# Norm of the output rows moved from a closing stage into the expert blocks

## The chip, the cores and the metric

The kernel runs on one core of one Trainium2 chip. The metric is the device time of one execution in microseconds (us). Three runs of the kernel before gave 2715.66, 2713.44 and 2708.99; the median is 2713.44.

Five engines work beside each other, each through its own instruction queue in order, and wait for each other on semaphores: TensorE (PE in the profile), VectorE (DVE), ScalarE (ACT), GpSimd (POOL) and SyncE (SP).

## The reference, cut to what matters

A decoder layer over 2048 tokens of width 1024. The change touches only what follows the router: a mixture of 16 experts, two per token, then the second LayerNorm.

```
dest = pad_start[s_e] + (arange(A) - start[s_e])        # rows sorted by expert, padded to blocks of 128
def expert_block(args):
    xb, e = args
    h = jax.nn.silu(xb @ w_gate[e]) * (xb @ w_up[e])    # 128x1024 @ 1024x512, twice
    return h @ w_down[e]                                # 128x512 @ 512x1024
out = segment_sum(y_sorted * s_w[:, None], s_tok)       # each token: two rows summed
x = layer_norm(DN_ALPHA * x + g2 * ffn, ln2_g, ln2_b)   # mean, variance, scale, bias per row
```

Each token has rows in exactly two expert blocks. Its sum is complete when the later of them has been added.

## The kernel before, in words

Everything up to the router is unchanged and is left out here. The last stage is `experts_and_norm` (L1711). Its input is `u2_rows` (the rows for the experts), `acc` in HBM (already holding x, and 128 spare rows behind the 2048) and `records`: for each place of a block the token number and its gate weight.

The blocks: 128 rows each, numbered 0 to total-1 over all experts; with these inputs there are 41 blocks and none of the 16 experts is empty. Each product is made in three matmuls (high by high, high by low, low by high parts of the float32 operands), so weights and rows are split in a high part by ScalarE (a copy to fp32r) and a low part by VectorE (a subtraction).

PE, per block b: wait for `x_lo_done`, gate and up product (48 matmuls, `p_gu`), `turn_x(b+1)` (8 transposes of the next block's rows, L1873), `down` (24 matmuls for block b-1, `p_y`), then 4 transposes of h (L1915). The down product of a block is thus made one block later (`down(b)` works on the h of block b-1), and DVE evicts its result in `evict` (L2072) at the start of the block after that, scaled by the gate weight in the record.

ACT, per block (`body`): `high_h` (L1966), wait for the gate product, two Silu (L1979), `high_x(b+1)` (L1972), and in the first block of an expert `split_dn` (L1955, 4 chunks, each waiting for `down`'s chunk). After the last block of an expert `split_gu` of the next expert follows (L1946, 8 chunks).

DVE, per block: `low_h` (L2062), `evict`, two products of h (L2089), `low_x(b+1)` (L2079, which posts `x_lo_done`), in the first block `split_dn` (L2050); `split_gu` (L2043) after the last block of an expert.

POOL, per loop turn b: wait for the evicted rows `y_out`, scatter-add them into `acc` (L1823, an indirect DMA), wait for `x_turned` and gather the next rows `x_raw` (L1800, an indirect DMA), wait for both transfers, shift the `record` slots (four small copies, L1796), load the next record (L1790).

SP loads expert weights in pieces as soon as the splits have freed the raw buffer `stay`.

The closing stage: when the last scatter-adds have landed, SP loads all 16 tiles of 128 rows back from `acc` into `stay` (L1784). DVE takes the moments (L2131, L2133), subtracts the mean and multiplies by the gain (L2118); POOL makes the reciprocal deviation (L1856, L1858) and adds the bias (L1849); ACT scales (L2023), takes the moments of four tiles, and stores (L2001).

## Time and profile before

| what | us |
|---|---|
| median of three runs | 2713.44 |
| profiled execution, its own time | 2713.14 |
| its span, first to last instruction | 2711.5 |
| PE busy in the span | 2491.6 (92%) |
| DVE busy | 1443.4 (53%) |
| ACT busy | 1123.4 (41%) |
| POOL busy | 842.7 (31%) |
| mean granted TensorE clock | 0.965 of full speed |

The span is what the trace covers; the execution's own time is 1.6 us longer. The page divides the span in 40 slices of 68 us; PE reads 9 tenths in nearly all of them, and 0 in the last, which is the closing stage. In the timelines the first number is the start in us from the span's start, the second the duration; "x8" is eight instructions merged in one row, and what stands in brackets is the idle time of that engine before the row and who ended it.

### The profile page before, as it was taken

What the parts mean: (1) busy time and instruction counts of PE and PEld (TensorE: products, weight loads), DVE (VectorE), ACT (ScalarE), POOL (GpSimd) and SP (SyncE); (2) the same over time, 40 slices, a digit from 0 to 9 for tenths busy, and PEclk for the clock granted to TensorE, in tenths of its full rate; (3) what the DMA queues carried; (4) which work ended last, traced back from release to release, by engine and by line L of the source; (5) the groups of instructions that cost most, each with busy time, mean ns of one, the idle gap of its engine ahead of it and who ended that gap; (6) DMA issues with size and microseconds to landing.
All of it is one profiled execution on the core that took longest, in us unless ns stands there. A gap on an engine that the chain in (4) does not pass through costs nothing. (4 is left out here: it accounts for less than half of the span.)

```text
span 2711.5 us, 35984 instructions
## 1 busy us (share of the span) xinstructions
PE 2491.6 (92%) x12505; PEld 2081.0 (77%) x12506; DVE 1443.4 (53%) x1871; ACT 1123.4 (41%) x1846; POOL 842.7 (31%) x692
## 2 busy tenths in 40 slices
PE   5999899999999999999989989994998999999990
PEld 4788678778888888888878877884787888888780
DVE  6122156665656566665654335775446545534755
ACT  3122144554544444454542012212556545534754
POOL 2111023452222222222221345665322222322326
PEclk9999999999999999999999999996999999999995
DMA  7699676767575666585537666532567646555847
GB/s 265 232 312 314 250 231 189 250 199 233 184 224 165 227 186 218 173 270 183 171 122 239 213 182 210 187 117 108 164 180 228 207 135 204 169 145 146 266 122 263
DMA packets 258254, 548.04 MB, mean 202 GB/s; under 512 B 23716, under 2 KB 93464, under 8 KB 257496
## 3 DMA queue, kind: packets, MB, share of 16 engines
q1 hardware_dynamic: 236072, 483.07, 53.7%
q0 software_dynamic: 14720, 45.04, 7.6%
q10 hardware_dynamic: 7344, 18.35, 1.7%
q8 instruction: 73, 1.20, 0.2%
q14 instruction: 45, 0.37, 0.0%
HBM read 393.37 MB, written 153.02 MB: 202 GB/s over the span
## 5 line engine op out<-in xcount | busy, mean ns | idle before, releaser
L93 PE MATMUL mx_acc<-u_u,mx_w_hi 128*128 128x512 f32 x1792 | 571.4, 400 | 1.5 <-DMA mx_w_lo<-halves 1.5
L722 POOL TENSOR_TENSOR mx_wt<-mx_wt,mx_rest 128x127 f32<-128x127 f32 (+15 forms) x128 | 271.5, 2121 | 741.5 <-DVE mx_rest L924 741.5
L93 PEld LDWEIGHTS mx_acc<-u_u,mx_w_hi 128*128 128x128 f32 x1792 | 326.1, 190 | 65.9 <-DMA mx_w_lo<-halves 1.9
L932 DVE TENSOR_TENSOR mx_wt_lo<-mx_p_t,mx_wt_hi 128x512 fp32r<-128x512 f32 (+2 forms) x320 | 192.1, 604 | 326.4 <-ACT mx_wt_hi L887 324.5
L93 PE MATMUL mx_acc<-u_u,mx_w_lo 128*128 128x512 f32 x896 | 352.8, 394 | 0.0
L887 ACT ACTIVATE mx_wt_hi<-mx_p_t 128x512 fp32r<-128x512 f32 (+2 forms) x320 | 170.8, 534 | 405.4 <-PE mx_p_t L774 359.3
L924 DVE TENSOR_TENSOR_SCAN mx_rest<-mx_rest,mx_zero 128x128 f32<-128x128 f32 (+15 forms) x128 | 315.8, 2467 | 8.6 <-ACT mx_wt L869 8.6
L93 PE MATMUL moe_p_gu<-keep_wide_hi,moe_x_hi 128*128 128x512 f32 x656 | 262.6, 400 | 14.1 <-DVE keep_wide_lo L2043 13.0
L93 PE MATMUL moe_p_gu<-keep_wide_hi,moe_x_lo 128*128 128x512 f32 x656 | 258.1, 393 | 0.0
L93 PE MATMUL moe_p_gu<-keep_wide_lo,moe_x_hi 128*128 128x512 f32 x656 | 257.9, 393 | 0.0
L868 ACT ACTIVATE mx_rest<-mx_p_z 128x512 f32<-128x512 f32 (+2 forms) x320 | 171.0, 534 | 100.0 <-PE mx_p_z L761 58.9
L93 PEld LDWEIGHTS mx_acc<-u_u,mx_w_lo 128*128 128x128 f32 x896 | 169.8, 189 | 38.8
L774 PE MATMUL mx_p_t<-keep_ident,mx_wt 128*128 128x128 f32 x1088 | 174.5, 275 | 22.3 <-POOL mx_wt L722 15.7
L774 PEld LDWEIGHTS mx_p_t<-keep_ident,mx_wt 128*128 128x128 f32 x1088 | 134.2, 141 | 77.8 <-POOL mx_wt L722 32.7
L869 ACT ACTIVATE mx_wt<-mx_p_z 128x512 f32<-128x512 f32 (+2 forms) x320 | 171.9, 537 | 0.0
L93 PE MATMUL fr_acc<-u_u,fr_w_hi 128*128 128x512 f32 x512 | 162.0, 398 | 6.5 <-DVE fr_stage L424 6.3
L2043 DVE TENSOR_TENSOR keep_wide_lo<-keep_stay,keep_wide_hi 128x1024 fp32r<-128x1024 f32 x124 | 142.3, 1218 | 36.5 <-ACT keep_wide_hi L1946 22.3
L2089 DVE TENSOR_TENSOR moe_h<-moe_p_gu,moe_act_g 128x256 f32<-128x256 f32 x82 | 30.9, 419 | 235.8 <-ACT moe_act_g L1979 235.8
L93 PEld LDWEIGHTS moe_p_gu<-keep_wide_hi,moe_x_hi 128*128 128x128 f32 x656 | 124.8, 190 | 40.0 <-DVE keep_wide_lo L2043 13.7
L760 PE MATMUL mx_p_z<-mx_k_hi,mx_q 128*128 128x512 f32 (+2 forms) x320 | 131.2, 410 | 16.6 <-DMA mx_q<-qk_lo 11.9
L93 PEld LDWEIGHTS moe_p_gu<-keep_wide_hi,moe_x_lo 128*128 128x128 f32 x656 | 124.7, 190 | 27.1
L93 PEld LDWEIGHTS moe_p_gu<-keep_wide_lo,moe_x_hi 128*128 128x128 f32 x656 | 125.0, 191 | 25.1
(257 smaller groups left out, 5130.2 us busy)
## 6 DMA issues: line engine op xcount, KB each, us to landing
mx_w_hi<-halves SPq DMA_DIRECT2D x98, 512.0 KB, 3.8
mx_w_lo<-halves SPq DMA_DIRECT2D x98, 512.0 KB, 5.2
keep_stay<-in_w_gate SPq DMA_DIRECT2D x64, 512.0 KB, 5.3
keep_stay<-in_w_up SPq DMA_DIRECT2D x64, 512.0 KB, 6.4
keep_stay<-in_w_down SPq DMA_DIRECT2D x32, 1024.0 KB, 6.7
u_saved<-u_u SPq DMA_DIRECT2D x4, 4096.0 KB, 19.5
mx_w_mod<-in_w_ada SPq DMA_DIRECT2D x64, 256.0 KB, 5.2
gate_t<-mx_g_out SPq DMA_DIRECT2D x64, 256.0 KB, 5.1
```

Source lines behind the costliest of these rows:

```text
L93: mm = pe.matmul(out, a, b, start=first and n == 0, stop=last and n == len(pairs) - 1, skip_group_check=True)
L722: pool.tensor_tensor(wt[:, t % 2, 0:w - 1], wt[:, t % 2, 0:w - 1], rest[:, t % 2, 1:w], ALU.mult).then_inc(m["weights_done"], 1)
L760: pe.matmul(out, q, hi, start=True, stop=False, skip_group_check=True)
L774: mm = pe.transpose(p_t[:, n % TR, (j - 4 * r) * P:(j - 4 * r + 1) * P], wt[:, t % 2, j * P:(j + 1) * P], ident[:])
L868: act.activation(rest[:, t % 2, a:b], p_z[:, n % ZB, 0:b - a], ACT.Sigmoid, scale=-SCALE)
L869: act.activation(wt[:, t % 2, a:b], p_z[:, n % ZB, 0:b - a], ACT.Sigmoid, scale=SCALE).then_inc(m["z_used"], 1)
L887: act.activation(to, p_t[:, n % TR, 0:(k - j) * P].rearrange("p (j t) -> p j t", t=P), ACT.Copy).then_inc(m["hi_done"], 1)
L924: dve.tensor_tensor_scan(x[:, ::-1], x[:, ::-1], zero[:].to_broadcast([P, w]), 1.0, ALU.mult, ALU.max).then_inc(m["scan_done"], 1)
L932: dve.tensor_tensor(wt_lo[:, first:first + k - j], p_t[:, n % TR, 0:(k - j) * P].rearrange("p (j t) -> p j t", t=P), f32(wt_hi[:, first:fi ...
L2043: dve.tensor_tensor(lo, raw, f32(hi), ALU.subtract).then_inc(m["gu_lo_done"], 1)
L2089: dve.tensor_tensor(h[:, w], p_gu[:, 1, w], act_g[:, w], ALU.mult).then_inc(m["h_done"], 1)
```

## The change

POOL's loop now does more. In turn b it scatters a finished tile of rows into `out` (`store_rows`), scatter-adds the evicted rows as before, gathers the next x rows as before, makes the reciprocal deviation of the row tile that DVE has just measured (`deviation`), shifts seven record slots (two copies with a second buffer `shifted`), loads the next record, and gathers the rows that the block's scatter-add has just completed in `acc` back into SBUF (`gather_rows`). ACT scales that tile inside `body`, between the two Silu and `high_x`. DVE takes its moments and centres it between `evict` and the products of h, and adds the bias between `low_x` and `split_dn`. A token's row is thus normed and stored after each of its two blocks; the second store overwrites the first. The closing stage of 16 tiles is gone; three tiles of rows are still finished after the last block. The stage's buffers (`rows`, 16 semaphores `rows_in`, the tile moments) go, `row_in`, `row_out`, `last_in`, `last_out` take four strips of 1024 columns of `stay` that the weights leave free.

```diff
+            def add_rows(slot, done):
+                pool.indirect_dma_start(out=acc, out_offset=at(slot), in_=y[:], in_offset=None, compute_op=ALU.add).then_inc(done, 16)
+            def gather_rows(slot, to, done):
+                pool.indirect_dma_start(out=to, out_offset=None, in_=acc, in_offset=at(slot)).then_inc(done, 16)
+            def store_rows(slot, rows, done):
+                pool.indirect_dma_start(out=out_rows, out_offset=at(slot), in_=rows, in_offset=None, bounds_check=S - 1,
+                                        oob_is_err=False).then_inc(done, 16)
+            def load_clear(n):
+                past(pool, m["scaled"], n)
+                pool.dma_start(row_in, acc[S:S + P, :]).then_inc(m["row_in"], 16)
+            def deviation(n):
+                wait_apart(pool, marks["pool"], m["row_mv"], n)
+                pool.tensor_scalar(var[:, 0:1], mv[:, 0, 1:2], EPS / ALPHA ** 2, None, ALU.add).then_inc(m["row_var"], 1)
+                wait_apart(pool, marks["pool"], m["row_var"], n)
+                pool.tensor_tensor(rstd[:, 0:1], var[:, 0:1], minus_half[:], ALU.pow).then_inc(m["row_rstd"], 1)
...
             for n in (1, 2, 3):
                 load_record(n)
+                record_known(n)
                 wait_apart(pool, marks["pool"], m["x_turned"], n)
                 gather_x(n)
...
                 shift_records(n)
+                if n > 1:
+                    deviation(n - 1)
+                    load_clear(n - 1)
...
-            with pool.Fori(0, total - 3) as b:
+            def block_rows(b, c=None):
+                if c is not None:
+                    wait_apart(pool, marks["pool"], m["normed"], b + 2)
+                    store_rows(0, row_out, m["out_stored"])
                 wait_apart(pool, marks["pool"], m["y_out"], b * 2 + 6)
-                add_rows(0, y, m["y_added"])
+                wait_apart(pool, marks["pool"], m["row_in"], b * 16 + 48)
+                add_rows(2, m["y_added"])
                 wait_apart(pool, marks["pool"], m["x_turned"], b + 4)
                 gather_x(b + 4)
+                if c is not None:
+                    wait_apart(pool, marks["pool"], m["out_stored"], c * 16 + 16)
+                pool.sem_inc(m["out_free"], 1)
+                deviation(b + 3)
                 wait_apart(pool, marks["pool"], m["y_added"], b * 16 + 16)
                 pool.sem_inc(m["y_free"], 1)
                 wait_apart(pool, marks["pool"], m["x_in"], b * 16 + 80)
                 shift_records(b + 4)
                 load_record(b + 5)
+                wait_apart(pool, marks["pool"], m["scaled"], b + 3)
+                gather_rows(1, row_in, m["row_in"])
+                record_known(b + 5)
+
+            block_rows(0)
+            block_rows(1)
+            with pool.Fori(0, total - 4) as c:
+                block_rows(c + 2, c)
...                                                     # POOL after the loop
+            store_rows(0, row_out, m["last_stored"])
+            add_rows(2, m["last_added"])
+            deviation(total + 1)
+            pool.wait_ge(m["last_added"], 16)
+            gather_rows(2, row_in, m["row_in"])
+            gather_rows(3, last_in, m["last_row_in"])
+            store_rows(1, row_out, m["last_stored"])
+            deviation(total + 2)
...
+            store_rows(2, row_out, m["last_stored"])
+            pool.wait_ge(m["last_stored"], 48)
+            store_rows(3, last_out, m["last_stored"])
...                                                     # ACT
+            def scale_rows(n):
+                act.wait_ge(m["row_rstd"], n + 1)
+                act.wait_ge(m["centered"], n + 1)
+                act.wait_ge(m["out_free"], n + 1)
+                act.activation(row_out, row_in, ACT.Copy, scale=rstd[:, 0:1]).then_inc(m["scaled"], 1)
             def body(b, e, first):
                 high_h(b)
...
                     act.activation(act_g[...], p_gu[...], ACT.Silu).then_inc(m["silu_done"], 1)
+                scale_rows(b)
                 high_x(b + 1)
                 if first:
                     split_dn(e, b)
...                                                     # DVE
+            def center_rows(n):
+                dve.wait_ge(m["row_in"], n * 16 + 16)
+                for i in range(2):
+                    dve.bn_stats(stats[:, 0, i], row_in[:, i * NB:(i + 1) * NB]).then_inc(m["row_stats"], 1)
+                wait_apart(dve, marks["dve"], m["row_stats"], 2 * n + 2)
+                dve.bn_aggr(mv[:, 0], stats[:, 0].rearrange("p a b -> p (a b)")).then_inc(m["row_mv"], 1)
+                dve.wait_ge(m["row_mv"], n + 1)
+                dve.scalar_tensor_tensor(out=row_in, in0=row_in, scalar=mv[:, 0, 0:1], in1=ln_g[:], op0=ALU.subtract,
+                                         op1=ALU.mult).then_inc(m["centered"], 1)
+            def add_bias(n):
+                dve.wait_ge(m["scaled"], n + 1)
+                dve.tensor_tensor(row_out, row_out, ln_b[:], ALU.add).then_inc(m["normed"], 1)
             def body(b, e, first):
                 low_h(b)
                 evict(b)
+                center_rows(b)
...
                 low_x(b + 1)
+                add_bias(b)
                 if first:
                     split_dn(e)
```

## Rows read from the trace of the kernel before

**Rows 1.** Busy time in one stretch of expert blocks: length, engines, clock, DMA share, GB/s.
```profile
2120.00:2400.00 280.00, 280.00 (x1331) 233.09 (x1330) 138.28 (x191) 147.50 (x196) 80.30 (x112) 1.00 0.60 177
```
**Rows 2.** Chain that ended last, one block and the start of the next.
```profile
2404.59 10.94 PE moe_p_gu L93 x48
2415.53 0.87 PE moe_p_x L1873 x8
...
2422.30 10.94 PE moe_p_gu L93 x48
```
**Rows 3.** Timeline of POOL in the same block.
```profile
2417.20 0.98 POOL L1800 DMA_INDIRECT keep_x_raw<-u_rows,keep_record  x1 [4.67 <-PE moe_p_x L1873]
2421.34 0.18 POOL L1796 COPY keep_record<-keep_record 128x2 uint32<-128x2 uint32 x1 [3.16 <-DMA keep_x_raw<-u_rows,keep_record]
...
2423.96 0.58 POOL L1790 DMA_DIRECT2D keep_record<-records  x1 [1.39 <-issue]
```
**Rows 4.** Timelines of ACT and DVE in the same block.
```profile
2416.44 1.09 ACT L1972 ACTIVATE moe_x_hi<-moe_p_x 128x512 fp32r<-128x512 f32 x2 [0.22 <-PE moe_p_x L1873]
...
2417.07 1.29 DVE L2079 TENSOR_TENSOR moe_x_lo<-moe_p_x,moe_x_hi 128x512 fp32r<-128x512 f32 x2 [0.33 <-ACT moe_x_hi L1972]
```
**Rows 5.** Closing stage: timeline of POOL, then groups by line (busy us, mean ns).
```profile
2673.60 0.21 POOL L1856 TENSOR_SCALAR moe_var<-moe_mv 128x2 f32<-128x2 f32 x1
2673.90 0.71 POOL L1858 TENSOR_TENSOR moe_rstd<-moe_var,moe_minus_half 128x2 f32<-128x2 f32 x1
...
L2118 DVE SCALAR_TENSOR_TENSOR keep_stay<-keep_stay,moe_mv,moe_p_gu 128x1024 f32<-128x1024 f32 x16 | 19.5, 1242 | 0.0
L2023 ACT ACTIVATE keep_stay<-keep_stay,moe_rstd 128x1024 f32<-128x1024 f32 x16 | 17.5, 1138 | 9.2 <-POOL moe_rstd L1858 8.6 <-DVE keep_stay L2118 0.6
L2131 DVE BATCH_NORM_STATS2 moe_stats<-keep_stay 128x6 f32<-128x512 f32 x24 | 15.3, 679 | 10.4 <-DMA keep_stay<-acc 10.4
```
**Rows 6.** Change of expert after a block that began at 2587.68: ACT, DVE.
```profile
2601.92 7.70 ACT L1946 ACTIVATE keep_wide_hi<-keep_stay 128x1024 fp32r<-128x1024 f32 x8
...
2603.01 9.17 DVE L2043 TENSOR_TENSOR keep_wide_lo<-keep_stay,keep_wide_hi 128x1024 fp32r<-128x1024 f32 x8 [1.57 <-ACT keep_wide_hi L1946]
```
**Rows 7.** An expert with one block, begun at 2053.93: ACT, then the chain.
```profile
2071.24 1.06 ACT L1955 ACTIVATE moe_dn_hi<-keep_stay 128x1024 fp32r<-128x1024 f32 x1 [0.30 <-PE moe_p_y L93]
...
2075.98 13.97 PE moe_p_gu L93 x48
```
**Rows 8.** TensorE clock behind three gaps: timeline of PE, then stretches (columns of Rows 1).
```profile
507.38 0.66 PE L774 MATMUL mx_p_t<-keep_ident,mx_wt 128*128 128x128 f32 x4 [2.23 <-POOL mx_wt L722]
580.53 0.33 PE L774 MATMUL mx_p_t<-keep_ident,mx_wt 128*128 128x128 f32 x1 [2.13 <-DVE mx_wt_lo L932]
...
507.40:510.40 3.00, 3.00 (x12) 2.43 (x13) 2.17 (x3) 1.57 (x3) 0.00 (x0) 0.68 0.43 129
580.50:583.50 3.00, 2.96 (x17) 2.52 (x18) 2.33 (x3) 2.46 (x5) 1.91 (x1) 1.00 0.00 0
2076.00:2082.00 6.00, 6.00 (x14) 4.74 (x15) 6.00 (x6) 5.98 (x7) 0.58 (x1) 0.50 0.96 350
```
**Rows 9.** DMA issues after 1900 (median us to landing), and the longest wait for x.
```profile
keep_x_raw<-u_rows,keep_record POOLq DMA_INDIRECT x40, 5.1
...
POOL keep_record L1796 <- DMA keep_x_raw<-u_rows,keep_record: 170.9, 41, 6.9
```
**Rows 10.** First block of the stage: POOL's gather for block 2, then the chain.
```profile
1908.48 1.00 POOL L1800 DMA_INDIRECT keep_x_raw<-u_rows,keep_record  x1 [2.33 <-DMA keep_record<-records]
...
1912.32 10.89 PE moe_p_gu L93 x48
```
**Rows 11.** The chain at the end of the last block, and the first scatter-add behind it.
```profile
2634.90 5.46 PE moe_p_y L93 x24
...
2643.92 6.02 DMA acc<-keep_early,keep_record
```
**Rows 12.** Timeline of POOL during VectorE's split of a new expert's weights.
```profile
2606.72 0.97 POOL L1796 COPY keep_record<-keep_record 128x2 uint32<-128x2 uint32 x1 [0.17 <-POOL keep_record L1796]
```

More of the change, by code:

```diff
@@ L1520, in _ @@
             pool.wait_ge(m["scattered"], 32 * NT)
[L1521 removed]
+            pool.dma_start(record[:, SLOTS - 1], records[bass.ds(start, P), :]).then_inc(ahead["record_in"], 16)
             gain(LAST)
@@ L1836, in _ @@
                 load_record(b + 5)
-            for i in range(2):
-                wait_apart(pool, marks["pool"], m["y_out"], total * 2 + 2 * i)
-                add_rows(0, y, m["last_added"])
-                wait_apart(pool, marks["pool"], m["last_added"], 16 * i + 16)
-                pool.sem_inc(m["y_free"], 1)
-                if i == 0:
-                    shift_records(total + 1)
-            pool.wait_ge(m["last_out"], 2)
-            add_rows(1, y_last, m["last_added"])
-            def add_bias(t):
-                pool.wait_ge(m["normed"], t + 1)
-                pool.tensor_tensor(rows[:, t], rows[:, t], ln_b[:], ALU.add).then_inc(m["res_done"], 1)
@@ L1851, in _ @@
-            pool.wait_ge(m["half_set"], 1)
-            for q in range(NT // 2):
-                a, b = 2 * q, 2 * q + 2
-                pool.wait_ge(m["mv_done"], b - upto(ACT_STATS, b - 1))
-                past(pool, m["act_mv"], 2 * upto(ACT_STATS, b - 1))
-                pool.tensor_scalar(var[:, a:b], mv[:, a:b, 1], EPS / ALPHA ** 2, None, ALU.add).then_inc(m["var_done"], 1)
-                pool.wait_ge(m["var_done"], q + 1)
-                pool.tensor_tensor(rstd[:, a:b], var[:, a:b], minus_half[:], ALU.pow).then_inc(m["rstd_done"], 1)
-                for t in range(max(0, a - 2), a):
-                    if t not in DVE_BIAS:
-                        add_bias(t)
@@ L1862, in _ @@
-            for t in (NT - 2, NT - 1):
-                if t not in DVE_BIAS:
-                    add_bias(t)
+                wait_apart(pool, marks["pool"], m["scaled"], b + 3)
[5 more added lines that the diff above has]
+                block_rows(c + 2, c)
+            wait_apart(pool, marks["pool"], m["normed"], total)
+            store_rows(0, row_out, m["last_stored"])
@@ L1990, in _ @@
             high_h(total)
-            act.wait_ge(m["h_done"], 2 * total)
-            act.wait_ge(m["x_lo_done"], total + 1)
-            for row, ps in ((ln_g, p_g), (ln_b, p_b)):
-                act.activation(ps, row[:], ACT.Copy).then_inc(m["rows_copied"], 1)
-            def store(t):
-                if t in DVE_BIAS:
-                    act.wait_ge(m["res_dve"], upto(DVE_BIAS, t))
-                else:
-                    act.wait_ge(m["res_done"], t + 1 - upto(DVE_BIAS, t))
-                act.dma_start(out_rows[t * P:(t + 1) * P, :], rows[:, t]).then_inc(m["stored"], 16)
@@ L2019, in _ @@
-            moments(ACT_STATS[0])
-            for t in range(NT):
-                act.wait_ge(m["rstd_done"], t // 2 + 1)
-                act.wait_ge(m["scaled"], t + 1)
-                act.activation(rows[:, t], rows[:, t], ACT.Copy, scale=rstd[:, t:t + 1]).then_inc(m["normed"], 1)
-                if t % 3 == 1 and t // 3 + 1 < len(ACT_STATS):
-                    moments(ACT_STATS[t // 3 + 1])
-                if t >= 5:
-                    store(t - 5)
-            for t in range(NT - 5, NT):
-                store(t)
@@ L2030, in _ @@
-            act.wait_ge(m["stored"], 16 * NT)
+            scale_rows(total)
+            scale_rows(total + 1)
+            act.wait_ge(m["last_rstd"], 1)
+            act.wait_ge(m["last_centered"], 1)
+            act.activation(last_out, last_in, ACT.Copy, scale=rstd[:, 1:2]).then_inc(m["last_scaled"], 1)
         @block.vector
@@ L2138, in _ @@
-            center(NT - 1)
-            add_bias(NT - 1)
+                dve.scalar_tensor_tensor(out=y_last[:, w], in0=p_y[:, n], scalar=record[:, 3, 1:2].bitcast(F32), in1=g2r[:, w],
+                                         op0=ALU.mult, op1=ALU.mult).then_inc(m["last_done"], 1)
+                if n == 0:
+                    add_bias(total)
+            center_rows(total + 1)
+            dve.wait_ge(m["last_row_in"], 16)
+            for n in range(2):
+                w = slice(n * NB, (n + 1) * NB)
+                dve.wait_ge(m["last_done"], n + 1)
+                dve.tensor_tensor(last_in[:, w], last_in[:, w], y_last[:, w], ALU.add).then_inc(m["last_summed"], 1)
+                dve.wait_ge(m["last_summed"], n + 1)
+                dve.bn_stats(stats[:, 1, n], last_in[:, w]).then_inc(m["last_stats"], 1)
@@ new lines, in _ @@
+            dve.wait_ge(m["last_stats"], 2)
+            dve.bn_aggr(mv[:, 1], stats[:, 1].rearrange("p a b -> p (a b)")).then_inc(m["last_mv"], 1)
+            add_bias(total + 1)
+            dve.wait_ge(m["last_mv"], 1)
+            dve.scalar_tensor_tensor(out=last_in, in0=last_in, scalar=mv[:, 1, 0:1], in1=ln_g[:], op0=ALU.subtract,
+                                     op1=ALU.mult).then_inc(m["last_centered"], 1)
+            dve.wait_ge(m["last_scaled"], 1)
+            dve.tensor_tensor(last_out, last_out, ln_b[:], ALU.add).then_inc(m["last_normed"], 1)
```

114 lines of the change are left out of this document (43 added, 71 removed).

## The prediction

> **What bounds the kernel now.** I read the engines' busy time in one stretch of the expert blocks first, then the chain that ended last, then the timelines of the three engines that feed PE. In 280 us of expert blocks PE is busy 280.00 us at the full clock, while DVE is busy 138.28, ACT 147.50 and POOL 80.30 us, and the DMA engines are busy 0.60 of the time [rows 1]. So there is room beside PE on each engine by sum. The chain shows the order: a block takes 17.71 us from one gate product to the next (2404.59 to 2422.30), all of it PE, and PE finishes the transposes of the next x at 2416.40, 11.81 us into the block [rows 2]. I write S for the start of a block's gate product and S+11.8 for this point. What has to be ready at S+17.71 is `x_lo`: ACT takes 1.09 us for `x_hi` (at S+11.85) and DVE ends `x_lo` at 2418.36, S+13.8 [rows 4]. So this hand-over has 3.9 us of slack, and only that. Behind the last block the closing stage stands alone: the last PE row of the last block's down product ends at 2640.36 [rows 11], the four transposes of h behind it take 0.44 (17.71 less the 17.27 that the gate product, the transposes and the down product take [rows 2, 11]), so the last block ends at E = 2640.80, and the span at 2711.5: 70.7 us.
>
> **Removed: the closing stage.** Of these 70.7 us a part comes back, since three tiles must still be finished. Counted from E, with the same durations: the loop's last turn gathers a row tile that lands at about E+8.3 (x gather at S+12.6, landing after 5.1 [rows 9]; shift and record 3.2, from 2421.34 to 2424.54 [rows 3], less 0.3 for two copies fewer; 0.3 to the next issue, another 5.1; 17.7 of it is the block's own). The scatter-add follows 0.8 later and takes 6.0 [rows 11]: E+15.1. Two gathers, 0.8 to start, 1.3 between them and 5.1 to land: the last sum is in at E+22.3, and the other tile, 1.3 us earlier, is centred meanwhile. DVE adds the last half rows and takes their moments, four steps of 0.65 and the aggregation with its waits, about 4.5 with the centring that is still running: E+26.8. Reciprocal deviation 1.1: E+27.9. ACT scales (1.14) and DVE adds the bias (1.25) [rows 5]: E+30.4 for the first of the two tiles, the second 2.5 later and under the first one's store. Then two stores follow one after the other, since the last waits for the one before: 2 x (0.8 + 6.0), at the scatter-add's price: E+44.1. The stage shrinks by 70.7 - 44.1 = 26.6 us. A plain scatter is not in the trace; with the gather's 5.1 for it the gain is 28.4, with the longest wait of 6.9 [rows 9] for each of the five transfers in the chain about 20. I take 26.6.
>
> **Added to each block: a longer way to x_hi.** ACT works in order, and `scale_rows(b)` stands between Silu and `high_x(b+1)`. It waits for `row_rstd`, which POOL posts in `deviation`, and POOL reaches `deviation` only behind `gather_x`, which waits for PE's transposes at S+11.81. From the rows: gather starts 0.80 behind the transposes (2417.20) and ends at S+13.59 [rows 3]; 0.17 for the waits between, the two small operations end 1.01 after they begin [rows 5], S+14.77; the scaling takes 1.14, S+15.93; x_hi and x_lo end 1.92 behind the start of x_hi [rows 4], S+17.87. That is 0.18 us later than PE wants it. In a plain block PE stalls 0.2 us; there are 23 such boundaries (40 boundaries in all, less 15 changes of expert and the first two): 4.6 us. Bounds for one: 0 when the deviation takes 0.2 less, 1.0 when POOL runs beside DVE and a step takes 0.97 where 0.18 is usual [rows 12].
>
> Behind `scale_rows` and `high_x` on ACT are `split_dn`, `split_gu` and the next block's `high_h`. On DVE `center_rows` (2 x 0.68, 0.2, 1.24 [rows 5]) stands before the products of h and `add_bias` (1.25) before the splits; DVE is idle there, and the products are due only at S+17.3, so I cost both at nothing. If the rows come later than S+14 that cover is gone.
>
> **Changes of expert.** Here the 3.9 us of slack were used. Before, x_hi was done at S+12.94 [rows 4], ACT's first new chunk began at S+14.24, 1.3 later, DVE's low part 1.09 behind it, and was ready about S+16.6 (2603.01 + 1.25) [rows 6], 1.1 us before PE came. Now x_hi is done at S+17.02 (S+15.93 + 1.09), and the same 1.3, 1.09 and 1.25 follow: S+20.7. PE stalls 20.7 - 17.7 = 3.0 us. The later chunks come every 1.15 us (9.17/8), faster than PE's 1.37 (10.94/8), so the stall is paid once. 12 of the 15 changes are of this kind: 36 us. Bounds 2.5 to 4.
>
> In the other three the expert has one block only, so `split_dn` stands between. Its fourth chunk ends at S+18.37 and PE waits until S+22.05 already now [rows 7], one of three such waits in the chain. With x_hi done only at S+17.02 the four chunks of 1.06 run end to end until S+21.3: 2.9 more, 8.7 us for three.
>
> **The clock behind the stalls.** After a stall of 4.3 us the next 6 us run at a granted clock of 0.50, which is 1.2 in place of 2.4 GHz [rows 8], and the 48 matmuls take 13.97 in place of 10.94 us [rows 7, 2], 3.0 more. After 2.23 us of idling the clock fell too (0.68 over 3 us), after 2.13 us it stayed at 1.00 [rows 8]. A stall of 3.0 us lies between: bounds 0 and 3.0, I take 1.4 for each of the twelve (one short fall more often than none) and 0.5 more for the three: 18.3 us.
>
> **Start of the stage.** In the first two blocks `deviation` is not behind `gather_x` alone but behind its landing and the shift. First boundary: gather at 1908.5 [rows 10], landing 4.4 later (4.1 in rows 3), 0.7 shift, 1.1 deviation, 1.14 scaling, 1.92 x_hi and x_lo: 1917.8 against 1912.3 [rows 10]: 5.5. Second: S+11.8, 0.8, 4.4, 0.7, 1.1, 1.14, 1.92, or S+21.9 against 17.7: 4.2. Clock behind both, 1.7 each: 3.4. Together 13.1 us.
>
> **POOL's loop.** It gets a gather of rows and a store. By the working above rows land at S+26.0, which is 8.1 into the next block. The scatter-add waits for them, then 0.8 and about 1.7 of issue (less than the 2 x 1.0 of two gathers [rows 3]), and is through at 10.6, 1.2 before x's transposes. With landings of 6.9 [rows 9] this is missed. I add 0.15 us for each of 38 blocks: 5.7. The DMA load rises from 0.60 by about a quarter; no term for it.
>
> **The sum.** 13.1 + 4.6 + 36 + 8.7 + 18.3 + 5.7 = 86.4 added, 26.6 saved: +59.8. On the profiled execution's own 2713.14 (0.3 below the median) that is 2773 us, 2.2% slower.
>
> **A price from the Trainium skill.** The x gather lands 5.1 us and the scatter-add 6.0 us after its issue [rows 9, 11]. By the Trainium skill, "DMA: Bandwidth & Descriptors", section "Anatomy of one DMA - SWDGE (gpsimd) path", a transfer from the GpSimd queue takes about 2.0 us plus its bytes over 436 GB/s; for 512 KB an estimate of 3.2 us. By it the five transfers of the last chain would take some 12 us less and the two gathers of the first blocks 3 less, and the time would be about 2758; the row has a duration and stands.
>
> **Rivals.** *The rows stay hidden.* If the deviation of a tile is ready before Silu ends (S+11.6), ACT never holds x_hi and only the closing stage counts: 2713.1 - 26.6 = 2686.5, faster. It speaks for it that each engine has idle time [rows 1], against it that POOL's order places `deviation` behind a semaphore of the same block. It decides from 3.9 us: the detour adds 4.1. Chance 0.06. *Some of the stall is hidden,* so that costs and the 26.6 cancel within 8 us: 0.03. *The clock holds.* PE stalls but the clock stays at 1.00, as after 2.13 us [rows 8]: 2773 - 21.5 = 2751. Chance 0.22. *The rows set the period.* If both gathers need 6.9 us, rows land 3.6 later, 11.7 into the block, and with 2.5 of scatter-add and 0.3 behind them POOL issues the gather of x at S+14.5, not 12.6: 1.9 more on each of 38 blocks, 72 us, 2845. For it speaks that the DMA share rises, against it the median of 5.1. Chance 0.12. *DVE holds POOL.* While DVE splits a new expert's weights a POOL copy took 0.97 in place of 0.18 [rows 12, 3], one DVE operation's length and no more. If the row gather at S+21 had to wait for the whole split (9.2 from S+19.4), rows would land some 13 us into the next block and x's gather slip by 3.2 us, 15 times: 48 us, 2821. Chance 0.07.
>
> The last is a rule of the Trainium skill: "SBUF - State Buffer", section "Who interferes with whom", says that a DVE instruction with two SBUF inputs and a GpSimd instruction that reads SBUF exclude each other for the whole instruction. By that rule one instruction is waited for, as the copy shows, and nothing is added; whether an indirect DMA's index reads wait behind a row of such instructions, no trace of before shows.
>
> **Numbers.** Forecast 0.50, 2773, its own range 2755 to 2800. The range of 8 in 10 takes in the forecast and the rivals at 2751 and 2821, leaves out the two below and most of the 2845: 2735 to 2830. About 0.3% (8 us) is what a measurement of this kernel tells from no change: faster 0.06, within it 0.03, slower 0.91.
>
> **What would show it.** Right: in ACT's timeline `x_hi` starts 4 us later in each block, behind a scaling that waited for POOL's pow; PE idles about 3 us, waiting for `keep_wide_lo`, at each change of expert, with the clock at 0.50 behind most; from the last block's end 44 us remain. Wrong: ACT's scaling starts right behind Silu, blocks still 17.71 us and changes of expert without a gap; or plain blocks near 20 us, with POOL's gather of x late behind the scatter-add.

## The result and the profile after

| | before | after |
|---|---|---|
| median (four runs each) | 2713.78 | 2804.61 |
| lowest to highest | 2708.99 to 2715.66 | 2802.99 to 2807.98 |
| profiled execution, its span | 2711.5 | 2801.5 |
| mean granted TensorE clock | 0.965 | 0.959 |
| PE's first transposes of the stage (1884.3 and 1885.8 in the span) to the end E of the last block | 756.5 | 875.4 |
| of it PE idle | 17.1 | 101.3 |
| of it PE busy | 739.4 | 774.2 |
| from E to the end | 70.7 | 40.3 |

The change is slower: ratio 1.0338, 95% interval 1.0325 to 1.035. The forecast was 2773, +60; measured are +91. The last three lines say where: 84.2 us more of idle PE, 34.8 us more of PE's busy time for the same products, 30.4 us less behind the last block.

The 34.8 us are in the main two things. The 41 gate products last 25.1 us longer in sum, since 17 of them take 12.5 to 14.1 us at a lower clock (3 before). The other 9.0 us are an overlap that is gone, which the next view shows.

First the page's busy times. PE shows 33 us more than before for the same products; DVE and POOL show what was added.

```profile
PE 2524.7 (90%) x12505; PEld 2099.5 (75%) x12506; DVE 1569.6 (56%) x2039; ACT 1131.8 (40%) x1844; POOL 906.5 (32%) x750
```

The chain over one plain block and the start of the next answers to [rows 2]. The block takes 18.05 us (2066.70 less 2048.65) and not 17.71, 0.34 more. Of that 0.11 is idle time ahead of the next gate product. The rest looks like a longer gate product (11.17 in place of 10.94), but is not one.

```profile
2048.65 11.17 PE moe_p_gu L94 x48
2059.83 0.87 PE moe_p_x L1911 x8
2060.70 5.46 PE moe_p_y L94 x24
2066.16 0.44 PE moe_p_h L1953 x4
2066.60 0.11 issue
2066.70 11.17 PE moe_p_gu L94 x48
```

In the timeline of PE before, the first matmul of the gate product starts at 2404.35, 0.24 us ahead of the end of the transposes of h (2404.59). The chain books these 0.24 us with the transposes, so [rows 2] has 10.94 for a product that lasts 11.18 from its first matmul's start. That overlap is there in 37 of before's blocks and in none of after's.

```profile
2403.99 0.60 PE L1915 MATMUL moe_p_h<-keep_ident,moe_h 128*128 128x128 f32 x4
2404.35 0.48 PE L93 MATMUL moe_p_gu<-keep_wide_hi,moe_x_hi 128*128 128x512 f32 x1
```

A change of expert, as in [rows 4, 6], in the timelines of POOL, ACT, DVE and PE. The block began at 2427.36, so S+11.8 is 2439.2. Read it from the top: the gather of x, the two small operations, the scaling that waited for `rstd`, only then `x_hi`, a table load of ScalarE, the first new chunk, its low part, and PE's first matmul, 2.83 us late.

```profile
2440.25 0.99 POOL L1800 DMA_INDIRECT keep_x_raw<-u_rows,keep_record  x1 [2.16 <-PE moe_p_x L1911]
2441.26 0.28 POOL L1819 TENSOR_SCALAR moe_var<-moe_mv 128x1 f32<-128x1 f32 x1
2441.73 0.58 POOL L1821 TENSOR_TENSOR moe_rstd<-moe_var,moe_minus_half 128x1 f32<-128x1 f32 x1 [0.18 <-POOL moe_var L1819]
...
2442.34 1.15 ACT L2017 ACTIVATE keep_stay<-keep_stay,moe_rstd 128x1024 f32<-128x1024 f32 x1 [3.10 <-POOL moe_rstd L1821]
2443.40 1.06 ACT L2010 ACTIVATE moe_x_hi<-moe_p_x 128x512 fp32r<-128x512 f32 x2
2444.48 1.28 ACT L1984 ACT_TABLE_LOAD   x1
2445.78 7.69 ACT L1984 ACTIVATE keep_wide_hi<-keep_stay 128x1024 fp32r<-128x1024 f32 x8
...
2446.87 9.17 DVE L2053 TENSOR_TENSOR keep_wide_lo<-keep_stay,keep_wide_hi 128x1024 fp32r<-128x1024 f32 x8 [0.44 <-ACT keep_wide_hi L1984]
...
2448.15 0.79 PE L94 MATMUL moe_p_gu<-keep_wide_hi,moe_x_hi 128*128 128x512 f32 x1 [2.83 <-DVE keep_wide_lo L2053]
```

The table load is most of the 1.3 us that the forecast counted between `x_hi` and the first chunk. It stands there in the kernel before as well (1.28 us at 2600.63), ahead of the split. In after it lies inside the delayed chain at each change of expert; no run here moves it.

The waits of the whole stage (total us, times, longest us) hold a second story. The first two rows are the predicted one. In the third, PE waits for `x_lo`: two of the nine are the start's gaps of 4.47 and 4.29 us, but the other seven lie in the middle of experts, where 0.2 us was forecast, and reach 3.6; the fourth shows POOL's scatter-add waiting up to 9.9 us for DVE's evict.

```profile
ACT keep_stay L2017 <- POOL moe_rstd L1821: 163.9, 39, 12.7
...
PE moe_p_gu L94 <- DVE keep_wide_lo L2053: 71.3, 15, 7.7
PE moe_p_gu L94 <- DVE moe_x_lo L2089: 24.7, 9, 4.5
...
POOL acc L1804 <- DVE keep_early L2082: 95.7, 15, 9.9
```

That story in POOL's timeline behind a change of expert: the scatter-add waits 7.75 us, since `evict` stands on DVE behind the eight chunks of the split. The gather of x still leaves at 2294.55, 12.9 us into its block, as in a quiet one; but it has to land before the record can be shifted and loaded and the rows be asked for. POOL then waits again for the rows, so that the next gather of x leaves at 2316.11, 16.4 us into the block that began at 2299.72, and the deviation behind it.

```profile
2292.49 1.59 POOL L1804 DMA_INDIRECT acc<-keep_early,keep_record  x1 [7.75 <-DVE keep_early L2082]
2294.55 1.00 POOL L1800 DMA_INDIRECT keep_x_raw<-u_rows,keep_record  x1 [0.46 <-issue]
...
2302.98 1.20 POOL L1791 COPY moe_shifted<-keep_record 128x12 uint32<-128x12 uint32 x1 [6.38 <-DMA keep_x_raw<-u_rows,keep_record]
2304.35 0.97 POOL L1793 COPY keep_record<-moe_shifted 128x12 uint32<-128x12 uint32 x1 [0.17 <-POOL moe_shifted L1791]
2306.84 0.66 POOL L1784 DMA_DIRECT2D keep_record<-records  x1 [1.52 <-issue]
2307.81 1.03 POOL L1807 DMA_INDIRECT keep_stay<-acc,keep_record  x1 [0.31 <-issue]
2312.88 1.02 POOL L1810 DMA_INDIRECT out<-keep_stay,keep_record  x1 [4.05 <-issue]
2314.21 1.59 POOL L1804 DMA_INDIRECT acc<-keep_early,keep_record  x1 [0.31 <-issue]
2316.11 0.99 POOL L1800 DMA_INDIRECT keep_x_raw<-u_rows,keep_record  x1 [0.30 <-issue]
```

The chain that ended last takes the same path with the landings in it. The x gather needs 8.26 us. SP has issued eight pieces of 512 KB of the next expert's weights from 2282.90 to 2290.15, and the second view (columns of [rows 1]) has the DMA engines busy 0.93 of the gather's time, moving 300 GB/s; beside the quiet gather at 2440.25 they move 201. The gate product that follows starts at 2321.29, behind a wait of 3.62 us for `x_lo`, and runs 12.74 us at the lower clock.

```profile
2294.55 8.26 DMA keep_x_raw<-u_rows,keep_record
...
2321.29 12.74 PE moe_p_gu L94 x48
```

```profile
2294.55:2302.80 8.25, 8.15 (x39) 6.56 (x38) 4.99 (x7) 6.14 (x8) 1.85 (x3) 1.00 0.93 300
2440.25:2444.30 4.05, 4.05 (x20) 3.35 (x19) 0.29 (x1) 1.96 (x3) 1.86 (x3) 1.00 0.79 201
```

Last the tail of the chain, where the store ahead of the last needs 3.54 us and not the scatter-add's 6.2. Behind the last store, issued at 2793.33, POOL's sequencer has a DRAIN row of 5.22 us (durations in ns, then the start) that ends the span.

```profile
2768.08 6.20 DMA acc<-keep_early,keep_record
...
2789.00 3.54 DMA out<-keep_stay,keep_record
```

```profile
L1714 POOLq DRAIN  x1: 5218/5218/5218, 2796.1 to 2796.1; - x1
```

### The profile page after: what moved, and what is told of

It reads as the page before. It is cut to its first block and busy times, and to the rows that moved or that the text cites. A ratio compares the mean times of both kernels' runs of the same rounds, so it can differ in the third digit from the quotient of the medians.

```text
span 2801.5 us, 36589 instructions
## 1 busy us (share of the span) xinstructions
PE 2524.7 (90%) x12505; PEld 2099.5 (75%) x12506; DVE 1569.6 (56%) x2039; ACT 1131.8 (40%) x1844; POOL 906.5 (32%) x750
## 3 DMA queue, kind: packets, MB, share of 16 engines
q1 hardware_dynamic: 233768, 474.68, 51.3%
## 5 line engine op out<-in xcount | busy, mean ns | idle before, releaser
L94 PE MATMUL moe_p_gu<-keep_wide_hi,moe_x_hi 128*128 128x512 f32 x656 | 273.8, 417 | 98.1 <-DVE keep_wide_lo L2053 71.3
L94 PE MATMUL moe_p_gu<-keep_wide_lo,moe_x_hi 128*128 128x512 f32 x656 | 268.3, 409 | 0.0
L94 PE MATMUL moe_p_gu<-keep_wide_hi,moe_x_lo 128*128 128x512 f32 x656 | 266.3, 406 | 0.0
L94 PEld LDWEIGHTS moe_p_gu<-keep_wide_hi,moe_x_hi 128*128 128x128 f32 x656 | 131.0, 200 | 135.4 <-DVE keep_wide_lo L2053 74.9
L775 PE MATMUL mx_p_t<-keep_ident,mx_wt 128*128 128x128 f32 x1088 | 174.3, 275 | 22.3 <-POOL mx_wt L723 15.8
L94 PEld LDWEIGHTS moe_p_gu<-keep_wide_hi,moe_x_lo 128*128 128x128 f32 x656 | 130.8, 199 | 29.2
L94 PEld LDWEIGHTS moe_p_gu<-keep_wide_lo,moe_x_hi 128*128 128x128 f32 x656 | 131.1, 200 | 26.8
L2089 DVE TENSOR_TENSOR moe_x_lo<-moe_p_x,moe_x_hi 128x512 fp32r<-128x512 f32 x84 | 54.1, 685 | 168.0 <-ACT moe_x_hi L2010 168.0
```

The costliest lines, as they stand in the source:

```text
L94: mm = pe.matmul(out, a, b, start=first and n == 0, stop=last and n == len(pairs) - 1, skip_group_check=True)
L775: mm = pe.transpose(p_t[:, n % TR, (j - 4 * r) * P:(j - 4 * r + 1) * P], wt[:, t % 2, j * P:(j + 1) * P], ident[:])
L2089: ins = dve.tensor_tensor(x_lo[part], p_x[:, n].rearrange("p (k t) -> p k t", t=P), f32(x_hi[part]), ALU.subtract)
```

## The experiments

All are edits of the kernel after, but for one. "Idle" is PE's idle time between its first transposes of the stage and E, "busy" the rest of that stretch, "tail" from E to the end, all three from one profiled execution each. Each ratio is to the kernel before as timed beside that run: 2713.4 for e1 to e4, 2712.0 for e5 to e8, 2713.9 for e9 to e11.

| kernel | idle | busy | tail | median | ratio to before, 95% |
|---|---|---|---|---|---|
| before | 17.1 | 739.4 | 70.7 | 2713.8 | 1 |
| after | 101.3 | 774.2 | 40.3 | 2804.6 | 1.0338 (1.0325 to 1.035) |
| e1 deviation early | 79.5 | 764.9 | 41.4 | 2774.5 | 1.0224 (1.0203 to 1.0246) |
| e2 scaling late | 63.4 | 755.3 | 41.3 | 2748.9 | 1.0131 (1.011 to 1.0152) |
| e3 rows early | 85.2 | 766.8 | 43.4 | 2782.3 | 1.0255 (1.0233 to 1.0277) |
| e4 = e1 + e3 | 70.3 | 761.1 | 42.7 | 2756.2 | 1.0153 (1.0133 to 1.0172) |
| e5 = e1 + e2 | 59.6 | 757.7 | 41.4 | 2749.8 | 1.0136 (1.0119 to 1.0153) |
| e6 before, with a delay on ACT | 49.2 | 754.1 | 72.6 | 2762.5 | 1.0182 (1.0162 to 1.0202) |
| e7 = e1 + e2 + index aside | 30.2 | 744.1 | 40.1 | 2699.9 | 0.9942 (0.9923 to 0.9962) |
| e8 few rows moved | 83.9 | 769.1 | 42.8 | 2780.1 | 1.0242 (1.0225 to 1.0259) |
| e9 index aside alone | 76.0 | 769.5 | 41.5 | 2774.5 | 1.0222 (1.0205 to 1.024) |
| e10 = e2 + index aside | 51.3 | 750.3 | 41.3 | 2728.8 | 1.0055 (1.0038 to 1.0072) |
| e11 = e1 + index aside | 47.6 | 750.6 | 40.0 | 2725.3 | 1.0043 (1.0028 to 1.0058) |

**e1, the deviation ahead of the gather of x.** POOL makes the deviation before it waits for PE's transposes.

```diff
                 add_rows(2, m["y_added"])
-                wait_apart(pool, marks["pool"], m["x_turned"], b + 4)
-                gather_x(b + 4)
                 if c is not None:
                     wait_apart(pool, marks["pool"], m["out_stored"], c * 16 + 16)
                 pool.sem_inc(m["out_free"], 1)
                 deviation(b + 3)
+                wait_apart(pool, marks["pool"], m["x_turned"], b + 4)
+                gather_x(b + 4)
```

> In POOL's loop the deviation stands before the wait for x's transposes and the gather of x, not behind them; nothing else differs from the changed kernel (2804.6 us). If the detour through that gather is what holds x_hi on ScalarE, ScalarE's scaling starts right behind Silu, a plain block is back at 17.7 us, the gaps of 2.8 us at changes of expert are gone and those of 7.7 us are back at 4.3: 8 + 58 us of stalls and some 20 us of clock fewer. If the late rows then hide too in the slack of 3.9 us: about 2701. If late rows cost by themselves: 30 us more, about 2731. If the place of the deviation is not the cause: 2800 to 2805.

2774.5, 30 us less than after, and neither 2701 nor 2731: late rows cost more here than the 30 us expected. Its waits show where it stays: where the rows are in time the changes of expert lose their gap (10 waits in place of 15), but the remaining ones grow to 11.0 us, and PE waits for `x_lo` in 13 places.

```profile
PE moe_p_gu L94 <- DVE keep_wide_lo L2053: 49.7, 10, 11.0
...
PE moe_p_gu L94 <- DVE moe_x_lo L2089: 24.2, 13, 4.6
```

**e2, the scaling behind x_hi.** ACT no longer holds `x_hi` for the deviation.

```diff
-                scale_rows(b)
                 high_x(b + 1)
+                scale_rows(b)
```

> ScalarE scales the row tile behind x_hi, not before it; POOL is as in the changed kernel. If the cause is that x_hi stands in ScalarE's queue behind the scaling, plain blocks are back at 17.7 and the first two blocks lose nothing, but the splits of a new expert still stand behind the scaling, which ends at 15.9 us into the block: 1.3, 1.1 and 1.2 behind it make 19.5, so gaps of 1.9 in place of 2.8 us at changes of expert. 8 + 15 + 14 us and some clock fewer: about 2757. If the clock mostly stays up behind 1.9 us: about 2745. If the traffic or POOL's loop is the cause, not ScalarE's queue: above 2790.

2748.9, 55.7 us less, near the two values expected. The wait for `x_lo` is nearly gone (0.8 us in one place). The gap at a well-timed change is 1.85 us, since the scaling, whose deviation still comes behind the gather, now stands ahead of the first new chunk; the late ones are still there, and the longest wait, at a one-block expert, is 8.1.

```profile
PE moe_p_gu L94 <- DVE keep_wide_lo L2053: 56.3, 15, 8.1
...
PE moe_p_gu L94 <- DVE moe_x_lo L2089: 0.8, 1, 0.8
```

**e3, the rows asked for ahead of the record's shift.** The gather of rows no longer stands behind the landing of x and the record's load. As it still reads its index from `record`, the shift now waits for the rows.

```diff
+                wait_apart(pool, marks["pool"], m["scaled"], b + 3)
+                gather_rows(2, row_in, m["row_in"])
                 wait_apart(pool, marks["pool"], m["x_in"], b * 16 + 80)
+                wait_apart(pool, marks["pool"], m["row_in"], b * 16 + 64)
                 shift_records(b + 4)
                 load_record(b + 5)
-                wait_apart(pool, marks["pool"], m["scaled"], b + 3)
-                gather_rows(1, row_in, m["row_in"])
-                record_known(b + 5)                  # now ahead of the next turn's gather_x
```

> The deviation stays where it was. The gather of the summed rows is issued before the wait for x (from slot 2, before the shift), and the wait for the record stands only before the next gather of x, so the rows do not wait for x's landing, the shift and the record load. If the 30 us of gaps beyond the plain ones come from this chain of landings: gaps of 2.8 at all twelve changes, none above but the three of one block, about 2767. If the landings are long because of the traffic and moving them wins nothing: 2795 to 2805.

2782.3, 22.3 us less, between the two values expected: the move wins, but does not bring all rows in time. Four changes of the common kind still idle 3.4 to 4.6 us.

**e4, e1 and e3 together.**

> Both moves of POOL's loop: deviation before the gather of x, rows gathered before the wait for x. If late rows are hidden once the detour is gone, the same as the deviation's move alone (about 2701, within 5). If they cost by themselves, 30 us less than that one. Below 2713 it beats the kernel before; the start of the stage still loses some 13 us with its clock.

2756.2, far above 2701: late rows are not hidden once the detour is gone. The two gains, 30.1 and 22.3, add up to nearly the 48.4 measured, so they are two costs and not one seen twice.

**e5, e1 and e2 together.**

> The deviation's move on POOL (2774.5 us by itself) together with the scaling behind x_hi on ScalarE (2748.9 by itself). The deviation is ready before x_hi is, so in a block whose rows are in time the scaling runs from 12.9 to 14.1 us and a new expert's first chunks are ready at 17.7: the gaps of 1.86 us of the second kernel go. 5 changes of expert and the first blocks are not touched by that: about 2735. If what is left is all late rows, so that the deviation's place no longer matters: 2745 to 2750.

2749.8, no different from e2 alone (2748.9), as the second value expected has it. With the scaling behind `x_hi` and the rows late, the place of the deviation on POOL is worth nothing more. What is left is the late rows: e7, which brings them in time, takes another 49.9 us off.

**e6, the detour alone, on the kernel before.** Four copies of 128x1024 stand on ACT between Silu and `high_x`, with no POOL and no DMA in them. The closing stage stays.

```diff
+                for i in range(4):
+                    act.activation(flat(stay, 1)[:, (KF + i) * D:(KF + i + 1) * D], ln_g[:], ACT.Copy).then_inc(m["idled"], 1)
                 high_x(b + 1)
```

> The kernel before, with four copies of 128x1024 (some 4.15 us) on ScalarE between Silu and x_hi in each block; no other work, transfer or wait is added and the closing stage stays. It measures the detour alone. If the slack of 3.9 us is the whole of that cost: plain blocks at 17.9, gaps of 2.9 at twelve changes of expert and 2.9 more at three, and the clock behind them, 5 + 35 + 9 + 18: about 2780. If the gaps in the changed kernel come from POOL, DVE or traffic and not from ScalarE: below 2725.

2762.5, 50.5 over before. The 2780 expected were for copies of 4.15 us, longer than the slack of 3.9; in the timeline of ACT the copies take 3.90 us and `x_hi` starts that much later. Plain blocks stay whole; twelve changes of expert idle 2.36 us each and the three one-block experts 6.43, again waiting for the weights' low part.

```profile
2409.07 3.90 ACT L1983 ACTIVATE keep_stay<-moe_ln_g 128x1024 f32<-128x1024 f32 x4
2412.86 1.08 ACT L1972 ACTIVATE moe_x_hi<-moe_p_x 128x512 fp32r<-128x512 f32 x2
```

Idle 32.1 more, busy 14.7 more. So the mechanism of the forecast at changes of expert, a later `x_hi` that moves the split of the next expert, is shown by itself, with no work of POOL or DVE and no transfer of the norm in it.

**e7, all three moves.** e1 and e2, and the row gather early as in e3 but with its index copied aside, so that the shift doesn't wait for the rows.

```diff
+                wait_apart(pool, marks["pool"], m["scaled"], b + 3)
+                pool.tensor_copy(held[:], record[:, 2]).then_inc(m["held_set"], 1)
+                wait_apart(pool, marks["pool"], m["held_set"], b + 1)
+                pool.indirect_dma_start(out=row_in, out_offset=None, in_=acc,
+                                        in_offset=bass.IndirectOffsetOnAxis(ap=held[:, 0:1], axis=0)).then_inc(m["row_in"], 16)
                 wait_apart(pool, marks["pool"], m["x_in"], b * 16 + 80)
                 shift_records(b + 4)
                 load_record(b + 5)
```

> As the first kernel of this call, and POOL gathers the summed rows before it waits for x, with the row numbers copied aside (one more small copy), so that the shift of the records does not wait for the rows. Scaled rows and landings no longer stand in one chain with x's landing, shift and record. If late rows are the rest: only the gaps of the three experts with one block stay, about 2700, faster than the kernel before. If the landings under the load of expert weights still come too late: 2720 to 2735.

2699.9, as expected, against 2712.0 for the kernel before beside it: 12 us (0.6%) faster, the ratio's whole interval below 1. Not every late gap is gone: four changes idle 0.6 to 3.6 us, and two of the three one-block experts 5.7 and 7.6 in place of 4.3. The chain shows the block back at 17.70 us, and in ACT's timeline `x_hi` starts 0.04 behind PE's transposes, with the scaling after it.

```profile
2428.98 10.94 PE moe_p_gu L94 x48
2439.91 0.87 PE moe_p_x L1915 x8
...
2446.68 10.94 PE moe_p_gu L94 x48
```

```profile
2440.82 1.09 ACT L2014 ACTIVATE moe_x_hi<-moe_p_x 128x512 fp32r<-128x512 f32 x2 [0.22 <-PE moe_p_x L1915]
2441.79 1.15 ACT L2021 ACTIVATE keep_stay<-keep_stay,moe_rstd 128x1024 f32<-128x1024 f32 x1
```

In this order the change costs PE 17.8 us in all up to E (774.3 less 756.5; 13.1 of it idle), and the tail gives 30.6 back. The other 101 of the change's 119 us up to E came from the order of the work.

**e8, the transfers nearly empty.** In the loop the row gather and the store move 16 of 128 rows; the other rows of the output are left out. Order and instructions stay.

```diff
-                gather_rows(1, row_in, m["row_in"])
+                pool.indirect_dma_start(out=row_in[0:16], out_offset=None, in_=acc,
+                                        in_offset=bass.IndirectOffsetOnAxis(ap=record[0:16, 1, 0:1], axis=0)).then_inc(m["row_in"], 16)
```

> The changed kernel, but in POOL's loop the gather of the summed rows and the store move 16 of 128 rows (the other rows of the output are left out); all waits and operations stay. If the traffic of these two transfers is what makes x's rows land late, x lands as before (median 5.1 or less) and the late gaps of 30 us go with their clock: about 2765. If it is the order of the waits: x's landing stays at 5.4, rows come 1 to 2 us sooner, 2785 to 2800.

2780.1, 24.5 less than after, between 2765 (traffic) and 2785 (order). The issues (KB left out; count, median us to landing) show e8 first, then after. The two shrunk transfers: 3.6 against 5.4 for the rows, 2.7 against 3.4 for the store. The x gather is back at 5.1 (5.4 in after), the value before, and what moved is its landing in the first block of an expert: the median of these 15 is 6.7 us in after, 5.4 in e8 and 5.7 before, against 4.3 to 4.4 in the other blocks of all three. So the added transfers do lengthen the gather of x, and just there. How much of the 24.5 us is that, and how much the two transfers' own landings in the serial chain, e8 doesn't separate.

```profile
keep_x_raw<-u_rows,keep_record POOLq DMA_INDIRECT x42, 5.1
...
keep_stay<-acc,keep_record POOLq DMA_INDIRECT x41, 3.6
out<-keep_stay,keep_record POOLq DMA_INDIRECT x41, 2.7
```

```profile
keep_x_raw<-u_rows,keep_record POOLq DMA_INDIRECT x41, 5.4
...
keep_stay<-acc,keep_record POOLq DMA_INDIRECT x41, 5.4
out<-keep_stay,keep_record POOLq DMA_INDIRECT x41, 3.4
```

**e9, e10, e11, one thing at a time with the rows in time.** e9 is after with the early gather and the index aside alone; e10 has the scaling late as well, e11 the deviation early as well. Their edits are those above.

> The changed kernel with one part of the fastest one (2699.9 us): the summed rows are gathered before the wait for x, with the row numbers copied aside; the deviation stays behind the gather of x and the scaling before x_hi. If the 30 us of gaps beyond 2.8 us and their clock come from the chain of landings: every change of expert of the common kind has a gap of 2.8 us, about 2766. If the detour alone makes nearly all of the loss, so that late rows matter only with it: 2790 or more.

> The fastest kernel with the deviation back behind the gather of x. Scaling stands behind x_hi, so PE has x in time, but a new expert's split waits for the scaling until 15.9 us: gaps of 1.86 us at twelve changes, some more at three, little clock: 2699.9 + 22 + 5, about 2727. If the rows' chain was all, and the place of the deviation is worth nothing once the rows are in time (as between 2748.9 and 2749.8): 2700 to 2705.

> The fastest kernel with the scaling back before x_hi on ScalarE. With the deviation early and the rows in time the scaling stands ready behind Silu and costs x_hi 1.1 us of its 3.9 us of slack: changes of expert of the common kind without a gap; only the first two blocks lose, as in the changed kernel, some 12 us with the clock: about 2712. If the scaling's place matters in every block: 2725 or more.

e9 takes 2774.5 (expected 2766), 30.1 less than after: this is what the late rows cost in the changed kernel. PE's waits for `x_lo` fall from 24.7 to 7.9 us and from 9 places to the 2 of the start, and nine of the twelve changes of the common kind idle 2.83 to 2.88 us, near the 3.0 forecast (the other three 3.3 to 3.7).

```profile
PE moe_p_gu L94 <- DVE keep_wide_lo L2057: 59.6, 15, 7.8
...
PE moe_p_gu L94 <- DVE moe_x_lo L2093: 7.9, 2, 4.4
```

e11 (2725.3) and e7 (2699.9) differ by the scaling ahead of `x_hi`: 25.4. e10 (2728.8) and e7 differ by the deviation behind the gather: 28.9. With both the cost is 74.7 (e9), 20.4 more than the two alone. With the deviation in time the scaling holds `x_hi` for its own 1.15 us; with the scaling behind `x_hi` the late deviation moves only the split, and the gap at a change is 1.9 us. e10 came out as expected (2727). e11 is 13 us above the 2712 expected: changes of the common kind are not all free of a gap (five idle 1.7 to 4.9 us).

The traces show where most of the 20.4 lie: some 15 are in the intervals between blocks of one expert. Only with both delays is the detour longer than the slack in every block, so that each plain block loses its 0.34 us; in e10 and e11 alike the gate product still overlaps the transposes of h in 25 blocks. And behind the twelve changes of the common kind the clock fell ten times in e9, four times in e10 and twice in e11.

After, e1, e2, e5, e7, e9, e10 and e11 have each of the three delays (deviation late, scaling ahead of `x_hi`, rows late) on and off, and the other two pairs behave otherwise. From e7's 2699.9, late rows alone cost 49.9 (e5). With the scaling ahead of `x_hi` they cost 74.6 (e1), nearly the sum of the two, 75.3. With the deviation late as well they cost 49.0 (e2), where the sum would be 78.8: the late rows hide the late deviation.

## Why the prediction was right or wrong

The time came out above the forecast's own range of 2755 to 2800 and inside the wider one of 2735 to 2830. The path that it named is the one that costs most; 31.6 us were missing, and about 24 of them in one term.

**Right: the longer way to x_hi, and where it hurts.** PE idles 2.80 to 2.83 us at seven changes of expert of the common kind, in place of none; forecast were 3.0. Five more hold the same and late rows on top. The three one-block experts wait 7.7 us in place of 4.34, 3.4 more each; forecast 2.9. The start has gaps of 4.47 and 4.29 us (forecast 5.5 and 4.2). e6 shows the mechanism with nothing else in it, e7 shows most of the gaps going when the detour goes.

**Right in size once the rows are in time.** e9 has 58.9 us more PE idle time than before. The forecast's idle terms without the one for POOL's loop are 9.7 for the start, 4.6 for the plain blocks, 36 and 8.7 for the changes, or 59.0; e9 has 9.2, 3.1, 36.3 and 10.3. That the sum agrees to 0.1 is luck. The twelve changes reach 36.3 only because three of them still hold some late rows, and the plain block was priced at 0.2 us (the working's own steps add up to 0.12) where it loses 0.34, of which two thirds do not count as idle. That overlap, 9.0 us over 37 blocks, stands in the busy time and not in the idle sum, and the forecast had no term for it at the changes of expert.

**Wrong: the step on POOL's loop.** "I add 0.15 us for each of 38 blocks: 5.7." e9 puts it at 30.1. The working took one turn of the loop in a quiet block and asked whether rows at 8.1 us into the block (8.3 by its own sum) are in time; they are, and quiet blocks do lose nothing. It didn't take the turn behind a change of expert. There the gather of x lands 5.2 to 8.3 us after its issue, the next weights in flight beside it, where a quiet one takes 4.0 to 4.4; the same places before had 4.2 to 7.8. The forecast named the longest wait of 6.9 us for this landing and priced it at 0.15 us a block. Shift, record, rows, moments and deviation follow in series behind that landing, and the scatter-add, held until 10.9 us into the block by the evict behind DVE's 9.2 us of splitting, isn't early either. The sentence "The DMA load rises from 0.60 by about a quarter; no term for it" left out a second part of this: e8 shows that the added transfers lengthen just these gathers (median 6.7 against 5.4).

Two rivals touched it. "The rows set the period" had the mechanism, but in every block, for 72 us; "DVE holds POOL" had the place, for 48. In after the chain runs through late rows in about a dozen blocks: seven waits of 1.6 to 3.6 us for `x_lo` in the middle of experts, 16.0 us, and five changes of expert with 4.6 to 7.1 in place of 2.8, 14.3 more. That is 30.3 us of idle time. (The seventh wait, 1.62 us at 2407.50, follows a deviation that waited 1.58 us for the landing of the store. e9 takes off 25.3 of idle time and 4.7 of busy time; its own late gaps are not quite gone.)

And 30.1 us is the price in this kernel alone. With the deviation ahead of the gather the same move is worth 49.2 (e1 less e11).

**The rule weighed as a rival.** By the forecast's reading of the Trainium skill ("SBUF - State Buffer", "Who interferes with whom") POOL's instruction waits for one DVE instruction. The trace agrees with that and no more: POOL's copies took 0.97 and 1.20 us in the turn shown and 0.19 in quiet ones, not the 9 us of a whole split. POOL's long wait, 7.75 us, is for the evict's semaphore, by order on DVE's queue.

**The clock: mechanism right, size near.** Forecast were 21.7 us for the clock. The gate products of e9, where the late rows are gone, last 20.2 us longer in sum than before's (485.0 and 464.8); in after, with more gaps, 25.1. Within e9 the terms differ from the forecast's: 3.1 for the start (forecast 3.4), 18.4 for the twelve changes (16.8), since the clock fell behind ten of them and not behind every second, and for the three one-block experts 1.4 less than before, not 1.5 more.

**The closing stage.** Forecast 26.6 less, measured 30.4. The stores were priced at the scatter-add's 6.0 for want of a row and land in 3.5, and the gathers at 5.1 where they land in 3.9 to 4.2; the last store is issued 32.1 us behind E, forecast 38.0. But behind its issue the span runs on for 8.2 us and not 6.0. The last 5.2 of them are POOL's DRAIN, which no term had: before, POOL's DRAIN of 7.87 us ended at 2709.4, ahead of ACT's end at 2711.3.

**The page's price.** By the Trainium skill ("DMA: Bandwidth & Descriptors", "Anatomy of one DMA - SWDGE (gpsimd) path") the forecast gave an estimate of 3.2 us for 512 KB. The measured medians are 5.4 for the gathers and 3.4 for the plain scatter, so it holds here for the scatter alone, and the row was the better price for the gathers.

**The rivals.** The clock did not hold. The stall was neither absent nor hidden: those two ask for the detour to be under 3.9 us, and only kernels with another order (e1, e11 and e7) get there where the rows are in time.

## What to carry to other kernels

Price an added stage in the worst turn of the loop and not in the median one: ask which queue is late, and which transfer lands late, when another stage's burst stands ahead of it, and follow the added serial chain (landing, shift, record, gather, moments) from that late start. When work is put into slack, what decides is whether an instruction on the critical engine waits for the added work: scaling behind `x_hi`, the deviation ahead of the gather and the index copied aside move no work away, and turned 91 us slower into 12 us faster. Delays that share one slack don't add up. Two can cost more together than each alone (74.7 against 54.3), and undoing one of them then takes off more than it costs by itself: moving the deviation is worth 49.2 from e9 and 28.9 as the last move. Or one hides the other, and undoing the hidden one shows nothing: the same move is worth nothing from e2 to e5. So test a move again after each of the others.

## What was unexpected in the hardware

**The clock behind short gaps.** The granted clock fell behind gaps as short as 1.9 us, but not behind all of one length (one profiled execution of each kernel). Behind the seven gaps of 2.8 us in after it fell three times; behind the nine of 2.83 to 2.88 in e9 eight times; behind the twelve of 2.36 in e6 six times; behind the nine of 1.87 to 1.95 in e10 three times. Two stretches of e6 behind gaps of 2.36 us each, with the columns of [rows 1], show the two cases: 14 matmuls in 3 us at 1.00, which is 2.4 GHz, and 7 at 0.50, which is 1.2 GHz.

```profile
2169.70:2172.70 3.00, 3.00 (x14) 2.47 (x15) 3.00 (x3) 3.00 (x4) 0.01 (x1) 1.00 0.22 37
2506.30:2509.30 3.00, 3.00 (x7) 2.33 (x8) 3.00 (x3) 3.00 (x4) 0.06 (x1) 0.50 0.25 57
```

The gap's length alone doesn't decide; what does stays open here.

**Indirect transfers of the same 512 KB differ by kind.** In after the median landing is 5.4 us for a gather, 6.2 for a scatter-add and 3.4 for a plain scatter. Single gathers of x lie between 3.9 and 8.3 us: their median is 6.7 in the first block of an expert, while the next weights load, and 4.3 elsewhere.
